# The second block's first projection: queries and keys computed with tokens on the partitions, head norm on 128x8 factors, then turned by the matmul engine; values stored to memory and read back

## The reference

```python
u = rmsnorm(h, norm_a_g[i])
proj = u @ w_in_a[i]                       # 1024 x 4112
q, k, v, f_logit, gate = jnp.split(proj, [1024, 2048, 3072, 3072 + 16], axis=-1)
q = rmsnorm(q.reshape(b, s, 16, 64), qnorm_a_g[i])
k = rmsnorm(k.reshape(b, s, 16, 64), knorm_a_g[i])
v = v.reshape(b, s, 16, 64)
log_f = jax.nn.log_sigmoid((f_logit + b_forget[i]).astype(jnp.float32))
o = fox_attention(q, k, v, log_f).reshape(b, s, 1024)
h = h + (o * jax.nn.silu(gate)) @ w_out_a[i]
```

## Time and profile before

| | |
|---|---|
| median of 3 runs | 3037.71 us (3036.03 to 3040.45) |
| profiled execution | 3037.1 us, span 3035.3 us |
| PE busy | 2561.3 us, 84% |
| PE weight loads busy | 2025.7 us, 67% |
| DVE busy | 1866.0 us, 61% |
| ACT busy | 1349.5 us, 44% |
| POOL busy | 828.9 us, 27% |
| mean granted clock of PE | 0.93 |

### The profile page before, as it was taken

How to read it: one execution, slowest core, us unless ns; L and a number is a source line. 1 busy time by engine, 2 the same in 40 slices (tenths; PEclk the granted TensorE clock), 3 DMA queues, 4 the chain that set the end, 5 groups by cost and what they waited for, 6 DMA issues and landing times. The chain is left out here.

```text
span 3035.3 us, 37631 instructions
## 1 busy us (share of the span) xinstructions
PE 2561.3 (84%) x13397; PEld 2025.7 (67%) x13397; DVE 1866.0 (61%) x2549; ACT 1349.5 (44%) x2313; POOL 828.9 (27%) x649
## 2 busy tenths in 40 slices
PE   1999799999768999999708989988885969878969
PEld 1786389787667888888507867766554756656547
DVE  5663555786338999999563299614444546852981
ACT  2353144784217888888443222225654132222540
POOL 0121012212003111111130033317776004531950
PEclk9999899999859999999859999989998979989989
DMA  5541000002039999999470011230003110013201
GB/s 213 170 153 28 0 1 1 1 29 84 30 139 413 405 414 409 415 419 411 162 276 22 21 35 43 62 132 29 29 29 118 42 56 28 28 46 123 96 8 49
DMA packets 144318, 392.35 MB, mean 129 GB/s; under 512 B 11835, under 2 KB 89760, under 8 KB 131762
## 3 DMA queue, kind: packets, MB, share of 16 engines
q1 hardware_dynamic: 131070, 345.69, 30.2%
q0 software_dynamic: 12096, 43.06, 3.5%
q10 hardware_dynamic: 1012, 1.72, 0.2%
HBM read 344.24 MB, written 46.20 MB: 129 GB/s over the span
## 5 line engine op out<-in xcount | busy, mean ns | idle before, releaser
L2435 POOL TENSOR_SCALAR fox_l<-fox_l,stat 128x256 f32<-128x256 f32 (+7 forms) x128 | 219.0, 1726 | 76.4 <-DVE stat L2471 76.4
L2463 DVE CUSTOM_DVE_ANT_0 fox_l<-PS,fox_c 128x256 f32<-128x256 f32 (+7 forms) x128 | 92.1, 756 | 155.3 <-PE PS L2517 110.0
L328 PE MATMUL PS<-uTh,wah 128*128 128x512 f32 x400 | 170.4, 426 | 0.0
L329 PE MATMUL PS<-uTl,wah 128*128 128x512 f32 x400 | 157.0, 393 | 0.0
L330 PE MATMUL PS<-uTh,wa_rest 128*128 128x512 f32 x400 | 156.8, 392 | 0.0
L2424 ACT ACTIVATE fox_l<-fox_l,stat 128x256 f32<-128x256 f32 (+7 forms) x128 | 98.4, 770 | 75.1 <-DVE stat L2463 75.1
L328 PE MATMUL PS<-xTh,wbh 128*128 128x512 f32 x288 | 121.4, 421 | 0.0
L2167 POOL TENSOR_SCALAR a_y<-a_corr 128x512 f32<-128x512 f32 x32 | 40.0, 1249 | 289.7 <-DVEq L2312 289.7
L2993 POOL TENSOR_SCALAR win_p<-win_p,stat 128x256 f32<-128x256 f32 (+1 forms) x128 | 110.7, 888 | 20.0 <-DVE stat L3044 20.0
L2299 DVE RECIPROCAL a_y<-a_y 128x512 f32<-128x512 f32 x32 | 107.2, 3349 | 10.0 <-ACT a_y L2227 9.8
L329 PE MATMUL PS<-xTl,wbh 128*128 128x512 f32 x288 | 112.6, 391 | 0.0
(11 more groups left out here) (529 smaller groups left out, 7896.2 us busy)
## 6 DMA issues: line engine op xcount, KB each, us to landing
we0g<-in_w_expert_gate SPq DMA_DIRECT2D x16, 2048.0 KB, 11.1
we0u<-in_w_expert_up SPq DMA_DIRECT2D x16, 2048.0 KB
we1g<-in_w_expert_gate SPq DMA_DIRECT2D x16, 2048.0 KB, 11.0
we0d<-in_w_expert_down SPq DMA_DIRECT2D x16, 2048.0 KB
we1u<-in_w_expert_up SPq DMA_DIRECT2D x16, 2048.0 KB
we1d<-in_w_expert_down SPq DMA_DIRECT2D x16, 2048.0 KB
wada_rest<-in_w_ada SPq DMA_DIRECT2D x16, 1024.0 KB, 5.2
wa<-in_w_in_a SPq DMA_DIRECT2D x25, 512.0 KB, 4.1
```

What stands on the lines that cost most here:

```text
L328: nc.tensor.matmul(out, lh, rh, start=start, stop=False)
L329: nc.tensor.matmul(out, lh, rl, start=False, stop=False)
L2435: nc.gpsimd.tensor_scalar(prob(p, e)[:, 0:K], prob(p, e)[:, 0:K], rsum[:, u % 8:u % 8 + 1], None, ALU.mult).then_inc(p_ready, 1)
L2463: nc.vector.tensor_tensor_reduce(out=prob(p, e)[:, 0:K], in0=PS[:, 2 * e:2 * e + 2, :].rearrange("p a b -> p (a b)")[:, 0:K], in1=C[:, h % ...
```

## The change

Stage 3 is turned round. It becomes 32 units of 4 column groups of 512 (two of queries, two of keys) x 8 token tiles; the token tile of u is stationary and the 512 columns of weights stream, as in the values' stage. A unit's result has tokens on the partitions and 8 heads of 64 along the free axis. ACT squares it from PSUM to PSUM (L2256 of the new file), DVE sums over each head's 64 values (`tensor_reduce`, 128x512 to 128x8), ACT takes the root of 128x8 factors, DVE does reciprocal and correction on 128x8 (five instructions) and multiplies the result by the factors, broadcast over each head, into a tile `qn` (L2351). PE turns the four 128x128 pieces (`turn`, L2390), and ACT evacuates them with the gain as a per-partition scale to `qa` or `ka` (L2247). POOL has no arithmetic left in the phase. The matmul by `pairs` is gone.

Weights for stage 3 now come as 4 groups of 512 columns (2 MB) in two tiles, each cast and subtracted in 4 pieces of 128x1024. Since their tiles take the place of `va`, the values are copied to a staging tile, stored to a new `v_dram` in 16 stores of 256 KB, and read back into `va` by 8 loads of 512 KB while stage 4 runs. The forget weights have a tile of their own. Stage 4 is as before, with chunks 0 to 2 loaded during the last group of stage 3.

`turn(u)` stands on PE behind the product of unit u+1, and the last one behind the first product of stage 4. The pieces of `forget` stand on DVE behind the multiplication of a unit rather than ahead of its reciprocal. The clearing of semaphores before the combine phase loses its barrier; a second clearing is added ahead of `phase_fox`. The tile of a helper of the first block's modulation (`acc_rest2`) is renamed `pad0`, and `qn` shares it.

```diff
@@ phase_combine
+    nc.clear_and_free_semaphores(env.spent)
@@ phase_a_projection, SP
-            for c in range(NCH):
-                if c >= 3:
-                    sp.wait_ge(mm, 2 * (c - 2))
-                sp.dma_start(ring[c % 3][:, :, :], chunk_of(w, slice(starts[c], starts[c] + P))
-                             ).then_inc(w_in[c % 3], 16)
+            sp.dma_start(wf[:, :, :], chunk_of(w, slice(3 * D, 3 * D + P))).then_inc(wf_in, 16)
+            group(0)
+            for u in range(2 * T):
+                i, t = u // T, u % T
+                sp.wait_ge(v_out, u + 1)
+                sp.dma_start(env.v_dram[t * P:(t + 1) * P, i * HALF:(i + 1) * HALF], stage[:, u % 4, :]
+                             ).then_inc(v_saved[u % 4], 16)
+            for i in range(4):
+                sp.wait_ge(v_saved[i], 64)
+            sp.wait_ge(f_mm, 2)
+            group(1)
+            for i in range(2, 4):
+                sp.wait_ge(mm, T * (i - 1))
+                group(i)
+            sp.wait_ge(mm, 3 * T)
+            for c in range(3):
+                gate_chunk(c)
+            sp.wait_ge(mm, 4 * T)
+            for t in range(T):
+                sp.dma_start(env.va[:, t, :], env.v_dram[t * P:(t + 1) * P, :]).then_inc(va_in, 16)
+            for c in range(3, KD):
+                sp.wait_ge(g_mm, 2 * (c - 2))
+                gate_chunk(c)
+            sp.wait_ge(va_in, 16 * T)
@@ POOL
-                nc.gpsimd.tensor_scalar(y[:, u % 2, :], corr[:, :], -0.5 / HD, 1.5, ALU.mult, ALU.add
-                                        ).then_inc(corr_used, 1)
-                pool.wait_ge(corr_used, u + 1)
-                nc.gpsimd.tensor_tensor(o, o, y[:, u % 2, :], ALU.mult).then_inc(normed, 1)
@@ ACT
+            for u in range(NU):
+                i, t = u // T, u % T
+                act.wait_ge(mm, u + 1)
+                if u >= 2:
+                    act.wait_ge(sums, u - 1)
+                nc.scalar.activation(PS[:, 3 + u % 2, :], PS[:, u % 3, :], ACT.Square).then_inc(squares, 1)
                 if u >= 1:
...
+                    evacuate(u - 1)
+                act.wait_ge(sums, u + 1)
+                if u >= 2:
+                    act.wait_ge(normed, u - 1)
+                nc.scalar.activation(stats(1, u), stats(0, u), ACT.Sqrt, bias=env.eps[:, 0:1], scale=1.0 / HD
+                                     ).then_inc(root, 1)
+                if i < 3 and 2 <= t < 6:
+                    group_hi(i + 1, t - 2)
@@ DVE
+            for u in range(NU):
+                i, t = u // T, u % T
+                ss, rs, nw = stats(0, u), stats(1, u), stats(2, u)
+                dve.wait_ge(squares, u + 1)
+                nc.vector.tensor_reduce(ss, heads(PS[:, 3 + u % 2, :]), AX_X, ALU.add).then_inc(sums, 1)
+                dve.wait_ge(root, u + 1)
+                do(nc.vector.reciprocal(rs, rs))
+                do(nc.vector.tensor_tensor(nw, rs, rs, ALU.mult))
+                do(nc.vector.scalar_tensor_tensor(nw, ss, EPS * HD, nw, ALU.add, ALU.mult))
+                do(nc.vector.tensor_scalar(nw, nw, -0.5 / HD, 1.5, ALU.mult, ALU.add))
+                do(nc.vector.tensor_tensor(rs, rs, nw, ALU.mult))
+                if u >= 2:
+                    dve.wait_ge(t_ready, u - 1)
+                nc.vector.tensor_tensor(heads(qn[u % 2][:, :]), heads(PS[:, u % 3, :]),
+                                        rs.unsqueeze(2).to_broadcast([P, GH, HD]), ALU.mult).then_inc(normed, 1)
                 if u % 2 == 0 and u < 14:
                     forget(u // 2)
...
+                if i < 3 and 2 <= t < 6:
+                    group_lo(i + 1, t - 2)
@@ PE
+            def turn(u):
+                pe.wait_ge(normed, u + 1)
+                if u >= 3:
+                    pe.wait_ge(t_out, u - 2)
+                elif u >= 1:
+                    pe.wait_ge(f_act, 1)
+                for c in range(4):
+                    last = nc.tensor.transpose(PS[:, 5 + u % 3, c * P:(c + 1) * P], qn[u % 2][:, c * P:(c + 1) * P],
+                                               env.ident)
+                last.then_inc(t_ready, 1)
...
+                if u >= 3:
+                    pe.wait_ge(normed, u - 2)
                 else:
                     pe.wait_ge(v_out, 2 * T - 3 + u)
...
+                    last = split_product(nc, PS[:, u % 3, :], (uh[:, k, tt], ul[:, k, tt]),
+                                         (wgh[i % 2][:, k, :], wgl[i % 2][:, k, :]), k == 0, k == KD - 1)
+                last.then_inc(mm, 1)
                 if u >= 1:
...
+                    turn(u - 1)
@@ build_program
-    nc.clear_and_free_semaphores(taken)
-    nc.all_engine_barrier()
+    env.spent = taken[:]
+    del taken[:]
     phase_combine(nc, A, env, sem)
```

More of the change, by code:

```diff
@@ L177, in setup @@
     env.csil = m.fixed("csil", [P, KD])
+    env.pad = [m.fixed(f"pad{i}", [P, HALF]) for i in range(2)]
 def col(env, name, k=0):
@@ new lines, in phase_a_projection @@
+    wg_in, wg_hi, wg_lo = [sem(f"wqk_in{i}") for i in range(2)], sem("wqk_hi"), sem("wqk_lo")
+    w_in, wh_done, wl_done, g_mm = [sem(f"wa_in{i}") for i in range(3)], sem("wah"), sem("wal"), sem("ag_mm")
+    bf_in, mm, squares, sums, root, normed = (sem("bf_in"), sem("a_mm"), sem("a_squares"), sem("a_sums"),
+                                              sem("a_root"), sem("a_normed"))
+    t_ready, t_out, dve_step = sem("a_t"), sem("a_t_out"), sem("a_dve")
+    v_mm, v_out, v_saved, va_in = sem("av_mm"), sem("av_out"), [sem(f"av_saved{i}") for i in range(4)], sem("va_in")
@@ L2250, in chunk_lo @@
                                         ringh[c % 3][:, :, :].bitcast(F32), ALU.subtract).then_inc(wl_done, 1)
-            for c in range(3):
-                chunk_lo(c)
+            dve.wait_ge(wf_hi, 1)
+            nc.vector.tensor_tensor(wfl[:, :, :], wf[:, :, :], wfh[:, :, :].bitcast(F32), ALU.subtract
+                                    ).then_inc(wf_lo, 1)
+            for piece in range(4):
+                group_lo(0, piece)
             fs = Steps(f_step)
@@ L2313, in _ @@
-            for c in range(4 + NU // 2, NCH):
-                chunk_lo(c)
+                if i < 3 and 2 <= t < 6:
+                    group_lo(i + 1, t - 2)
+                elif i == 3 and t in (2, 4, 6):
+                    gate_lo(t // 2 - 1)
+            for c in range(3, KD):
+                gate_lo(c)
         @block.tensor
@@ L2328, in _ @@
                 last.then_inc(v_mm, 1)
-            pe.wait_ge(wl_done, 1)
+            pe.wait_ge(wf_lo, 1)
             for n in range(2):
-                chunk_product(6 + n, 0, n).then_inc(mm, 1)
-            def head_sums(v):
-                pe.wait_ge(squares, v + 1)
-                if v >= 2:
-                    pe.wait_ge(normed, v - 1)
-                nc.tensor.matmul(PS[:, 4 + v % 2, :], env.pairs, sq[:, :], start=True, stop=True
-                                 ).then_inc(sum_mm, 1)
+                h = slice(n * HALF, (n + 1) * HALF)
+                for k in range(KD):
+                    last = split_product(nc, PS[:, 6 + n, :], (wfh[:, k, :], wfl[:, k, :]), (uh[:, k, h], ul[:, k, h]),
+                                         k == 0, k == KD - 1)
+                last.then_inc(f_mm, 1)
@@ new lines, in _ @@
+                h = slice(n * HALF, (n + 1) * HALF)
+                pe.wait_ge(wl_done, c + 1)
+                if g >= 4:
+                    pe.wait_ge(silu, g - 3)
+                else:
+                    pe.wait_ge(normed, NU - 1 if g == 0 else NU)
+                for k in range(KD):
+                    last = split_product(nc, PS[:, g % 4, :], (ringh[c % 3][:, k, :], ringl[c % 3][:, k, :]),
+                                         (uh[:, k, h], ul[:, k, h]), k == 0, k == KD - 1)
+                last.then_inc(g_mm, 1)
```

169 lines of the change are left out of this document (77 added, 92 removed).

## The result

| | before | after |
|---|---|---|
| median of all runs | 3038.64 us (4 runs, 3036.03 to 3040.45) | 3007.46 us (4 runs, 3002.84 to 3011.07) |
| ratio, 95% interval | | 0.9897 (0.988 to 0.9915) |
| span of the profiled execution | 3035.3 us | 3003.3 us |
| the changed phase, from the first product of the values to the attention's first matmul | 417.38 us | 387.58 us |

The change made the kernel 1% faster. The forecast was 3007.5 us. Of these, 28.3 are the queries' and keys' stage, 0.8 the gates' and 0.8 the products of values and forget gates, which the forecast left as it was.

The account below looks back on a forecast made before the run. PE's products plus sums were taken to bound the queries' and keys' stage, with DVE's chain right behind. 3037.1 - 27.0 (stage) - 1.4 (gates) - 1.6 (clearings) = 3007.1, given as 3007.5 us for the median; range 3000 to 3019.

Parts of the forecast that it names:

- Products: Queries' and keys' stage on PE: 32 x 24 matmuls before and after, operands exchanged, 174.1 us, no change.
- Sums off, transposes on: PE in the queries' and keys' stage: sums save 0.90 us a unit (28.8), four transposes add 0.50 (16.0).
- The 273 ns rival: Each transpose on PE costs its full duration: 35.0 us instead of 16.0, time 3026; chance 0.04.
- The chain: A unit's steps from Square to DVE's multiplication take 3.8 us, covered by PE's next product of 5.44 us.
- The large wait: PE waits 3.8 us after products 5 and 6, behind the third `forget` piece; clock loss 1.5 us.
- The first wait: Start of the queries' and keys' stage: PE waits 1.0 us for the first unit's chain, table load included.
- The stage: Queries' and keys' stage takes 196.4 us against 223.4, 27.0 us less.
- The gates: Gates' stage takes 87.0 us against 88.4, as the slow start behind the last wait goes: 1.4 us less.
- The DMAs: Stores and loads of the values, gate chunks and weight groups are all covered and cost nothing.
- The clearings: One barrier fewer ahead of the combine phase: 1.6 us less; the clearing ahead of the attention is hidden.
- The rival with more waits: DVE and ACT leave more PE waits, at units 2, 4, 10 and the first: about 12 us, 3019; chance 0.10.
- The slower rival: Chain through small DVE factors grows, as beside POOL's arithmetic (2.12 us a step): up to 3124 us; chance 0.03.

Follow-up runs that it names:

- a_turn8: The changed kernel with each unit's four transposes made twice, into the same bank: 3016.6 us.
- a_barrier: The changed kernel with the barrier behind the clearing of semaphores put back ahead of the combine phase: 3007.6 us, one execution.
- a_latev: The changed kernel with the eight loads of `va` issued behind the last product of the gates instead of the last of the keys: 3015.1 us.
- a_ kernels: Follow-up kernels made by editing the changed kernel, eight in all; measured from 2999.6 to 3045.7 us.
- b_ kernels: Follow-up kernels made by editing the kernel before the change, four in all; measured from 2995.6 to 3033.4 us.
- a_late: The changed kernel with eight POOL memsets between ACT's root and DVE's reciprocal in every unit, so DVE waits for them: 3045.7 us.
- a_lateturn: The changed kernel with eight POOL memsets per unit between DVE's multiplication and PE's transposes, so only PE waits for them: 3030.2 us.

## Why the prediction was right, step by step

*Time and sum.* 3007.5 against 3007.46. The closeness of the total is luck: the changed kernel's own runs spread over 8 us, and the profiled one took 3005.2 where the sum has 3007.1. The sum's parts say more.

*Products: no change.* Right. 5.91 - 0.47 is the 5.44 of before, with operands exchanged.

*Sums off, transposes on.* 0.90 off as counted, and 0.50 on as forecast: measured 0.47, which makes 1.0 us over 32 units. The 273 ns rival is out (a_turn8).

*The chain.* Forecast 3.8 us, measured 3.6. Both 128x512 passes took 0.69 us, the root 0.30, the small steps about 0.17 with 0.20 between starts; all as put down. DVE at half its work, right.

*The large wait.* Forecast 3.8 us, measured 3.5 (PE stands from 1751.8 to 1755.3). The clock loss behind it was forecast as 1.5 us. The changed kernel's trace has 2.9, with twelve matmuls at 1.2 GHz, but a_barrier and a_latev have 1.6 and 1.7 behind the same wait. So the forecast was within the scatter of executions, not plainly mis-sized; what makes the difference is open.

*The first wait.* Forecast 1.0 us, measured 0.2. I had put the table load behind the reduction. Rows of ACT and DVE, in order of time, show it beside it:

```profile
1718.77 1.28 ACT L2262 ACT_TABLE_LOAD   x1
1718.89 0.69 DVE L2342 TENSOR_REDUCE stat<-PS 128x8 f32<-128x512 f32 x1 [2.27 <-ACT PS L2256]
1720.07 0.30 ACT L2262 ACTIVATE stat<-stat,eps 128x8 f32<-128x8 f32 x1
```

*The stage.* 27.0 us less forecast with 32 turns in 196.4 us. Measured 195.1 with 31 turns inside, 195.6 with the last: 27.8 less. Against the forecast the first wait is 0.8 us shorter, the turns 1.0, the large wait 0.3, and the clock loss 1.4 longer: 0.7 in all.

*The gates.* Forecast 1.4 us less; 87.6 against 88.4 with the last turn in it, 0.8 less. The slow start is gone, as counted; the turn of 0.47 had been booked in the stage.

*The DMAs.* Free, as forecast. A group of 2 MB landed in 8.6 us, less than the 10.8 I had allowed; a_latev shows what the cover of the values is worth. The attention's first matmul comes 5.4 us behind the last product in both kernels, so the second clearing costs nothing.

*The clearings.* Forecast 1.6 us less, measured 1.2 in the gap, and a_barrier shows the cause. The size was near by luck: the rows it came from show a whole phase boundary, not a barrier.

*Not forecast.* Behind the phase the program took 1004.0 us instead of 1006.6. No work there was changed. Some of it is scatter: 1.3 of the 2.6 us stand at the attention's start, whose first product with `va` comes after 16.4 us here and after 17.6 before, but after 16.6 to 17.9 in the other a_ kernels. But the stretch took 1004.6 to 1006.2 us in the eight other a_ kernels and 1006.7 to 1008.1 in the four b_ kernels. The two ranges don't meet, so about a microsecond may belong to the change; what makes it is open.

*The rival with more waits.* It named three units with both a piece of `forget` and a weight rest, 2, 4 and 10; by the code unit 12 is a fourth. None of 2, 10 and 12 made a wait in the changed kernel.

*The slower rival.* Right to give it little, wrong in its sum. I had said that it would decide from 4.3 us more in the chain, by the rule of half a microsecond a unit. With 3.1 us more, a_late was already slower than before, and with the same delay outside DVE's order (a_lateturn) the time was 3030. The rule holds for the steady units of what only PE waits for (6.40 us against 6.33); for a delay in which DVE stands, DVE's own walk through the unit must fit too. And it leaves out the start and the large pieces of `forget`, where most of the rest was lost. POOL's effect on the small steps, the reason given for that rival, is real and small, about 2.5 us.

*What bounded the old stage.* "PE's products plus sums, with DVE's chain right behind" is what the three b_ kernels show, and more sharply: taking off one cost gave 21.2 or 5.7 us, both together 42.7. In the steady units DVE needed 0.3 us less than PE; PE's waits came with the forget gates' pieces on top.

## What to carry to other kernels

Where two engines stand at their limit side by side, a single edit shows only part of its worth, and the edit of the second one shows little until the first is made (here 5.7 of 21 us): try them together before either is dropped. Here the change of layout was one way to be rid of both costs, and not the cheapest: a one-pass sum and a function that gives the reciprocal root directly, with the correction step left in, did more in the old layout (phase 374.6 us, against 387.6 for the change and 382.6 with its one wait removed). A long instruction of small value (here 6.5 us over 16 partitions) is best cut to fit the room of several units, since one wait of 3.5 us cost another 1.6 to 2.9 in clock.

## What the runs showed of the hardware that I had not expected

A table load on ACT ran while the instruction that needs it still waited for its operand: it starts at 1718.77, as soon as the one before it ends, and the reduction that the root waits for ends at 1719.6. A DVE reciprocal of 128x8 was never held beside POOL's arithmetic (0.203 us in both), while the four other small steps were, so that one took up to 0.63 us instead of 0.17. The same wait of PE, 3.5 us, was followed by 2.9 us of loss at the lower clock in one execution and by 1.6 and 1.7 in two others with the same code in the stage. A float32 matmul of 128x512 in the rounded format cost PE 0.227 us where the unrounded one cost 0.90, four times as much, for the same shape.
